# A sixteenth 1 MB buffer for expert weights, in the tiles `ea` and `bg`, loaded in four pieces after the router

## The chip, the cores and the metric

One core of a Trainium2 chip runs the whole program. The metric is device time in microseconds of that core: the median of three runs, beside one more execution that the hardware profiler recorded, on which all rows here are read. The engines are PE (TensorE), DVE (VectorE), ACT (ScalarE), POOL (GpSimd) and SP (SyncE, which in this kernel issues nearly all loads). Each runs its own list of instructions in order, and they meet at semaphores. Sixteen DMA engines move the data.

## The reference

One decoder layer over 536 tokens (512 prompt tokens, 16 meta tokens ahead of them, 8 decode tokens), all in float32: four token mixers, gates and an output projection, and then a mixture of experts. The change touches the last part. Cut to it:

```python
def hier_moe(x, rg_w, rg_b, re_w, re_b, w1, w3, w2):
    pg = jax.nn.softmax((t @ rg_w + rg_b).astype(F32), axis=-1)
    pg_top, g_idx = lax.top_k(pg, 1)
    g_oh = jax.nn.one_hot(g_idx[:, 0], N_GROUPS, dtype=F32)
    le_sel = jnp.einsum('ng,nge->ne', g_oh, le)
    e_val, e_idx = lax.top_k(le_sel, TOP_K_IN)
    wts = jax.nn.softmax(e_val, axis=-1) * pg_top
    ...
    h = jax.nn.silu(jnp.einsum('nd,edf->nef', t, w1)) * jnp.einsum('nd,edf->nef', t, w3)
    h = h * gate[..., None].astype(h.dtype)
    return jnp.einsum('nef,efd->nd', h, w2).reshape(b, l, d)
```

There are 16 experts; w1 and w3 are 1024 x 256 each and w2 is 256 x 1024, so an expert has 3 MB of weights and all have 48 MB. Each of the 520 tokens that have an output goes to two experts.

## The kernel before

The program first projects and mixes, merges the branches, multiplies by the output weights (to 640 us), normalises and routes (to 667 us), and then runs the experts, which is the stage of this change.

**Experts.** They are taken in four quads of four (`QUADS`), a quad in three rounds (`ROUNDS`); a round is one PE tile, in which each expert of the quad has 32 rows of tokens and its own 32 rows of the array. Tokens are gathered by GpSimd from a copy in HBM (`gather`, into `cg`, `sgt`, `dqk`), transposed on PE (`rows_T`, L1198), multiplied by w1 and w3 (`hidden_one`, L1209), passed through silu and product (ACT L1673, DVE L2443), transposed (`hidden_T`, L1261) and multiplied by w2 (`outputs`, L1278, 32 matmuls for each of 3 rounds: 96 for a quad). ACT and DVE copy the result, times its gate, into `cst` (L1683, L2456), and GpSimd adds it to y in HBM, first choices as they come, second choices at the quad's end (L2644).

**Weights.** They are streamed in 48 loads of 1 MB, n = 0 to 47, twelve for a quad: j = n % 12 from 0 to 7 brings w1 and w3, each load for two experts and two of the eight slices of 128 input rows, and j = 8 to 11 brings w2 of one expert. SyncE issues them (`weights`, L505 for a whole MB in one DMA, L508 for the four quarters of a buffer that lies in pieces). With `STREAM` = 15 buffers, load n goes to buffer n % 15. The buffers are no memory of their own: they are tiles of the earlier stages (`kv`, `br`, `sgd` two each, `qb`, `vtok`, `qk` two, `tmp` two, `xn` two, and the fifteenth in four pieces, in `dv`, `vec` and the end of `vtok`), and the first fill has to wait until each tile has been given up. So it is issued in steps: n = 0 to 7 once the merges are done, 8 and 9 after the output product, 14 after two small outputs of the mixers have been stored, 10 and 11 once the first gathers have landed and the transposes out of `tmp` are done, 12 and 13 (in `xn`) once all five blocks of y's residual are stored (`y_out`).

**From n = 15 on** SyncE waits, in order, for the use of load n - 15 (`weights_used`): for the first six of a quad's loads a count that PE gives while it multiplies (`m_use`), for the seventh and eighth the end of the hidden product (`m_h1`), for w2 the end of the outputs (`m_y`). PE's own `weights(n)` waits for the landing (`m_w`).

**Around it.** The five residual blocks are written to y in HBM by SyncE (L521), out of `xn` and of `bg`; the router works in `ea` and `dr` and ends on DVE with the gates of the tiles (`g_w`, L2432), which gives `g_ok`. ACT and GpSimd wait for it too.

Of the kernel before, what the change touches and what calls it, by code (L numbers as in the profile page):

```python
# [14 lines left out]
KT = DM // P  # L15
# [23 lines left out]
RING = 6  # L39
STREAM = 15  # L40
LAST_OUT = [(3, 4), (5, 0), (6, 7)]
# [90 lines left out]
def program(nc, w_in, w_mg, w_dp, w_out, w_13, w_2, x_d, n2_d, xT_d, const_d, vec_d, ret0_d, gla0_d, kc, vc, pt, o):  # L132
    with ExitStack() as ctx:
# [3 lines left out]
        def sem(name):  # L137
            return ctx.enter_context(nc.semaphore(name))
# [15 lines left out]
        bg, cg, dr = sb("bg", 2 * T), sb("cg", 2 * T), sb("dr", 2 * T)  # L154
# [3 lines left out]
        ea = sb("ea", 1024)  # L158
# [124 lines left out]
        slot = [[t[:, g, :] for g in range(4)] for t in slot]  # L283
        slot.append([dv[:, 0:512], dv[:, 512:1024], vec[:, V_WA:V_WA + 512], vtok[:, 2048:2560]])
        xe = [view(t, 0, DM) for t in (cg, sgt, dqk)]
        xeT = [view(ring, DM * i, KT, P) for i in range(2 * ROUNDS)]
# [8 lines left out]
        ld_x, init_ok = [sem(f"ld_xt{i}") for i in range(4)], sem("init_ok")  # L295
# [35 lines left out]
        xs_ok, idx2_ok, oh_ok, oh2_ok, tab_ok, g_ok = [sem(k) for k in ("xs_ok", "idx2_ok", "oh_ok", "oh2_ok", "tab_ok", "g_ok")]  # L331
        m_w = [sem(f"m_w{i}") for i in range(STREAM)]
        m_xe, m_yst = [sem(f"m_xe{i}") for i in range(ROUNDS)], [sem(f"m_yst{i}") for i in range(ROUNDS)]
# [56 lines left out]
        def _(sp):  # L390
# [104 lines left out]
            def weights(n):  # L495
# [6 lines left out]
                w = n % STREAM  # L502
                if w < STREAM - 1:
                    whole = slot_whole[w].rearrange("p (e k) n -> p e k n", e=2) if j < KT else slot_whole[w]
                    sp.dma_start(whole, src).then_inc(m_w[w], 16)  # L505
                else:
                    for g in range(4):
                        sp.dma_start(slot[w][g], src[:, g // 2, g % 2, :] if j < KT else src[:, g, :]).then_inc(m_w[w], 16)  # L508

# [21 lines left out]
            sp.wait_ge(outs, 16 * POOL_OUTS)  # L531
            weights(STREAM - 1)
            for b in range(NB):
# [11 lines left out]
            weights(12)  # L545
            weights(13)
            for n in range(STREAM, 12 * QUADS):
                weights_used(n - STREAM)
                weights(n)
# [17 lines left out]
        def _(pe):  # L567
# [633 lines left out]
            def weights(n):  # L1201
                pe.wait_ge(m_w[n % STREAM], (64 if n % STREAM == STREAM - 1 else 16) * (n // STREAM + 1))
                return slot[n % STREAM]
# [1627 lines left out]
```

## Time and profile before

| | us |
|---|---|
| median of 3 runs | 829.5 |
| lowest, highest | 828.33, 832.01 |
| profiled execution, its own time | 832.47 |
| its span, first to last instruction | 830.7 |
| PE busy in the span | 783.2 (94%) |
| mean granted TensorE clock in the span | 0.969 |

The span is what the rows below are read in: their times count from its start. The rest of the profiled execution's time, 1.8 us, lies around it. A share of busy time says little here: PE is 94% busy over the whole, but what a change to the expert stage is worth is read at that stage's end. In a row of the chain or of a timeline the first number is the start, the second how long it took.

### The profile page before, as it was taken

How to read it: one execution, taken by the hardware profiler on the slowest of the kernel's cores; microseconds unless marked ns; L12 is line 12 of the kernel's file. 1: busy time of each engine (PE TensorE's matmuls, PEld its weight loads, DVE VectorE, ACT ScalarE, POOL GpSimd, SP SyncE). 2: the span in 40 equal slices, each digit the busy share in tenths (PEclk: the TensorE clock that was granted, in tenths of full speed). 3: DMA queues.
4: the chain of work that ended last, by engine and by line, in shares of the span. 5: the costliest groups of instructions: out<-in, count | busy, mean ns of one | idle time of the engine just before them, and what ended most of it. 6: DMA issues, size and time to landing. Idle time of an engine off the chain costs nothing.

```text
span 830.7 us, 14351 instructions
## 1 busy us (share of the span) xinstructions
PE 783.2 (94%) x5282; PEld 560.4 (67%) x5282; DVE 379.7 (46%) x741; ACT 223.7 (27%) x428; POOL 295.4 (36%) x220
## 2 busy tenths in 40 slices
PE   9999999989999999899999999999899799999981
PEld 8887777666667788677777778888688534333320
DVE  4671676767468578444444111635423712022110
ACT  4122424331413634113314224222101512011010
POOL 0000421244663874245435555433240113232313
PEclk9999999999999999899999999999899799999986
DMA  9242632245665542155534553332193779999923
GB/s 368 94 149 87 218 104 78 70 135 159 171 184 171 166 146 64 29 164 165 181 125 135 170 175 129 126 107 81 36 378 133 267 270 408 386 372 386 383 71 48
DMA packets 72154, 147.23 MB, mean 177 GB/s; under 512 B 13207, under 2 KB 47016, under 8 KB 70036
## 3 DMA queue, kind: packets, MB, share of 16 engines
q1 hardware_dynamic: 65716, 135.43, 46.8%
q0 software_dynamic: 5920, 10.82, 5.2%
q8 instruction: 42, 0.69, 0.3%
q14 instruction: 28, 0.23, 0.1%
q10 hardware_dynamic: 448, 0.06, 0.1%
HBM read 137.71 MB, written 18.90 MB: 189 GB/s over the span
## 4 chain that ended last, share of the span: by engine, by line
PE 78%; DVE 9%; SPq 5%; DMA 3%; issue 2%; ACT 2%; POOLq 0%; POOL 0%; ACTq 0%; DVEq 0%
PE ps L875 19%; PE ps L599 13%; PE ps L1209 7%; PE ps L844 6%; PE ps L1117 6%; PE ps L1278 4%; PE ps L614 4%; PE ps L642 3%; DMA br<-in_w 3%; SPq L505 2%; PE ps L899 2%; PE ps L674 2%; PE ps L588 1%; PE ps L1198 1%; PE ps L949 1%
## 5 line engine op out<-in xcount | busy, mean ns | idle before, releaser
L599 PE MATMUL ps<-xn,ring 128*128 128x268 f32 (+1 forms) x576 | 138.4, 395 | 1.0 <-ACT qb L1371 0.9
L599 PEld LDWEIGHTS ps<-xn,ring 128*128 128x128 f32 x576 | 108.2, 192 | 26.1 <-issue 3.4
L2531 POOL TENSOR_TENSOR kv<-kv,sgd 128x1024 f32<-128x1024 f32 (+1 forms) x32 | 81.1, 2548 | 119.7 <-DVE tmp L1820 70.2
L2644 POOL DMA_INDIRECT out_y<-cst,gtab x24 | 37.3, 1555 | 83.5 <-DVE cst L2456 43.2
L1514 ACT ACTIVATE sgt<-sgt,vec 128x260 f32<-128x260 f32 x60 | 30.0, 510 | 134.2 <-DVE sgt L2100 78.0
L844 PE MATMUL ps<-br,ring 128*128 128x260 f32 x256 | 61.7, 389 | 0.8 <-DVE sgt L2104 0.8
L875 PE MATMUL ps<-xn,qb 128*128 128x260 f32 x240 | 59.4, 392 | 0.0
L875 PE MATMUL ps<-xn,ring 128*128 128x260 f32 x240 | 57.9, 384 | 1.0 <-ACT tmp L1371 1.0
L844 PEld LDWEIGHTS ps<-br,ring 128*128 128x128 f32 x256 | 48.3, 192 | 12.1 <-issue 3.7
L875 PEld LDWEIGHTS ps<-xn,qb 128*128 128x128 f32 x240 | 46.5, 194 | 7.5
L875 PEld LDWEIGHTS ps<-xn,ring 128*128 128x128 f32 x240 | 45.1, 190 | 8.3 <-issue 1.4
L1853 DVE TENSOR_REDUCE sgd<-kv 128x32 f32<-128x1024 f32 (+1 forms) x32 | 40.5, 1279 | 9.7 <-POOL kv L2531 9.6
L2091 DVE TENSOR_TENSOR sgt<-ps,sgt 128x260 f32<-128x260 f32 x15 | 6.4, 427 | 71.8 <-PE ps L875 71.8
L2443 DVE TENSOR_TENSOR ring<-ring,ps 128x256 f32<-128x256 f32 x12 | 5.1, 421 | 71.1 <-ACT ring L1673 71.1
L2575 POOL TENSOR_TENSOR qb<-qb,ring 128x512 f32<-128x512 f32 x15 | 19.3, 1286 | 46.4 <-PE ps L875 46.4
L2570 POOL TENSOR_TENSOR qb<-ring 128x512 f32<-128x512 f32 x15 | 20.4, 1360 | 36.8 <-PE ps L875 36.5
L642 PE MATMUL ps<-ring,xn 128*128 128x128 f32 x256 | 31.4, 285 | 0.0
L642 PEld LDWEIGHTS ps<-ring,xn 128*128 128x128 f32 x256 | 30.9, 201 | 0.6 <-ACT tmp L1371 0.3
L2542 POOL TENSOR_TENSOR cst<-sgt,cst 128x520 f32<-128x520 f32 x16 | 20.6, 1289 | 29.7 <-ACTq L1524 29.7
L614 PE MATMUL ps<-kv,ring 128*128 128x268 f32 x128 | 29.9, 394 | 0.0
L1371 ACT ACTIVATE cst<-ps 128x520 f32<-128x520 f32 x32 | 19.3, 603 | 37.7 <-PE ps L844 37.7
L2582 POOL TENSOR_TENSOR qb<-ring,qb 128x512 f32<-128x512 f32 x15 | 19.3, 1287 | 27.8 <-PE ps L875 27.2
(506 smaller groups left out, 1527.4 us busy)
## 6 DMA issues: line engine op xcount, KB each, us to landing
ring<-in_w_mg SPq DMA_DIRECT2D x32, 640.0 KB, 4.7
kv<-in_kc SPq DMA_DIRECT2D x128, 128.0 KB, 2.1
kv<-in_vc SPq DMA_DIRECT2D x128, 128.0 KB, 2.2
ring<-in_w_in SPq DMA_DIRECT2D x24, 512.0 KB, 4.6
kv<-in_w SPq DMA_DIRECT2D x8, 1024.0 KB, 14.9
br<-in_w SPq DMA_DIRECT2D x7, 1024.0 KB, 18.5
sgd<-in_w SPq DMA_DIRECT2D x6, 1024.0 KB, 19.5
qk<-in_w SPq DMA_DIRECT2D x6, 1024.0 KB, 15.5
```

Of the source, the lines that this page charges most:

```text
L599: mm = pe.matmul(ps[:, 2 * (t % 2) + h, 0:hw], wsl(c, k), xnv[:, k, col0 + h * hw:col0 + (h + 1) * hw], start=(k == 0), stop=(k == KT - 1))
L614: mm = pe.matmul(ps[:, EARLY[name] + h, 0:HT], wsl(c, k), xgv[:, k, h * HT:(h + 1) * HT], start=(k == 0), stop=(k == KT - 1))
L642: pe.matmul(ps[:, 2 * (t % 2), b * P:(b + 1) * P], xnv[:, k, b * P:(b + 1) * P], wsl(c, k), start=(k == 0), stop=(k == KT - 1))
L844: mm = pe.matmul(ps[:, bk + h, 0:HN], wsl(CAT[f"G{n}{m}"], KT + k), brv[:, BR[n] + k, h * HN:(h + 1) * HN], start=(k == 0), stop=(k == 1))
L875: mm = pe.matmul(ps[:, bk, 0:HN], w[:, k * P:(k + 1) * P], x, start=(k == 0), stop=(k == 3))
L1117: mm = pe.matmul(ps[:, bk, 0:HN], wk, x, start=(k == 0 and i in (1, 2, 5)), stop=(k == 3), skip_group_check=(i in (6, 7, 4, 3)))
L1209: mm = pe.matmul(ps[rows, i % ROUNDS, :], xeT[i % (2 * ROUNDS)][:, k, rows], slot[(i // ROUNDS * 12 + k - k % 2 + g // 2) % STREAM][2 * (g ...
L1278: mm = pe.matmul(ps[rows, LAST_OUT[r][n] if last else 6 + n, :], hT[r][:, f, rows], w[g][2 * f + n], start=(f == 0), stop=(f == 1), tile_p ...
L1514: act.activation(g, g, ACT.Sigmoid, bias=vv(V_BM + 8 * "ABCD".index(n) + m + i)).then_inc(g_a, 1)
L1853: dve.tensor_reduce(row, kb.rearrange("p s (m d) -> p s m d", d=32), X, ALU.add).then_inc(k_used, 1)
L2531: pool.tensor_tensor(kb, kb, qbc[:, b:b + 1, :].to_broadcast([P, HALF // 2 + (half and u), 256]), ALU.mult)\
L2644: pool.indirect_dma_start(out=o["y"], out_offset=on_rows(to), in_=rows.rearrange("p a n -> p (a n)"), in_offset=None, bounds_check=N - 1, ...
```

## The change

`STREAM` becomes 16, and the number of whole buffers gets a name of its own, `WHOLE` = 14. The fifteenth buffer (index 14) stays as it is, and a sixteenth (index 15) is added, in four pieces of 256 KB: both halves of `ea`, where the decays of mixer D's gates and later the router's numbers were, and the first 1024 columns of `bg`, B's gate and later the fifth residual block. Load n = 15 is now part of the first fill. It is issued after n = 12 and 13, behind the wait for `y_out`, and behind one new wait of SyncE, for `g_ok`. From n = 16 on SyncE waits for the use of n - 16. The landing of the new buffer is counted on an old semaphore, `ld_x[0]`, which stands at 16 since the first load of the input, so PE's wait adds that base.

```diff
--- before.py
+++ after.py
@@ -37,7 +37,7 @@
 RB = N // NB
 WCH = 1280
 RING = 6
-STREAM = 15
+WHOLE, STREAM = 14, 16
 LAST_OUT = [(3, 4), (5, 0), (6, 7)]
 OUT_ORDER = [1, 5, 6, 2, 7, 3, 4]
 OUT_BANKS = [(6, 7, 3), (0, 1, 2)]
@@ -282,6 +282,7 @@
         slot_whole = slot
         slot = [[t[:, g, :] for g in range(4)] for t in slot]
         slot.append([dv[:, 0:512], dv[:, 512:1024], vec[:, V_WA:V_WA + 512], vtok[:, 2048:2560]])
+        slot.append([ea[:, 0:512], ea[:, 512:1024], bg[:, 0:512], bg[:, 512:1024]])
         xe = [view(t, 0, DM) for t in (cg, sgt, dqk)]
         xeT = [view(ring, DM * i, KT, P) for i in range(2 * ROUNDS)]
         si = [view(ring, 6 * DM + 256 * i, 256) for i in range(ROUNDS)]
@@ -329,7 +330,7 @@
         rw_ok, lg_t, lg_a, lg_d = sem("rw_ok"), sem("lg_t"), sem("lg_a"), sem("lg_d")
         r1, r2, sel_ok, idx_ok = sem("r1"), sem("r2"), sem("sel_ok"), sem("idx_ok")
         xs_ok, idx2_ok, oh_ok, oh2_ok, tab_ok, g_ok = [sem(k) for k in ("xs_ok", "idx2_ok", "oh_ok", "oh2_ok", "tab_ok", "g_ok")]
-        m_w = [sem(f"m_w{i}") for i in range(STREAM)]
+        m_w = [(sem(f"m_w{i}"), 0) for i in range(STREAM - 1)] + [(ld_x[0], 16)]
         m_xe, m_yst = [sem(f"m_xe{i}") for i in range(ROUNDS)], [sem(f"m_yst{i}") for i in range(ROUNDS)]
         m_t, m_ta, m_td, m_h1, m_si, m_h = [sem(f"m_{k}") for k in ("t", "ta", "td", "h1", "si", "h")]
         m_ht, m_htev, m_y, m_ya, m_yd, m_use = [sem(f"m_{k}") for k in ("ht", "htev", "y", "ya", "yd", "use")]
@@ -500,12 +501,12 @@
                 else:
                     src = w_2[4 * q + j - KT, :, :, :].rearrange("p f (h n) -> p (f h) n", h=2)
                 w = n % STREAM
-                if w < STREAM - 1:
+                if w < WHOLE:
                     whole = slot_whole[w].rearrange("p (e k) n -> p e k n", e=2) if j < KT else slot_whole[w]
-                    sp.dma_start(whole, src).then_inc(m_w[w], 16)
+                    sp.dma_start(whole, src).then_inc(m_w[w][0], 16)
                 else:
                     for g in range(4):
-                        sp.dma_start(slot[w][g], src[:, g // 2, g % 2, :] if j < KT else src[:, g, :]).then_inc(m_w[w], 16)
+                        sp.dma_start(slot[w][g], src[:, g // 2, g % 2, :] if j < KT else src[:, g, :]).then_inc(m_w[w][0], 16)
 
             def weights_used(n):
                 q, j = n // 12, n % 12
@@ -529,7 +530,7 @@
             weights(8)
             weights(9)
             sp.wait_ge(outs, 16 * POOL_OUTS)
-            weights(STREAM - 1)
+            weights(WHOLE)
             for b in range(NB):
                 sp.wait_ge(tt_a, b + 1)
                 sp.dma_start(scr_x[b * RB:(b + 1) * RB, :], tk[b]).then_inc(xs_ok, 16)
@@ -544,6 +545,8 @@
             sp.wait_ge(y_out, 16 * NB)
             weights(12)
             weights(13)
+            sp.wait_ge(g_ok, 1)
+            weights(STREAM - 1)
             for n in range(STREAM, 12 * QUADS):
                 weights_used(n - STREAM)
                 weights(n)
@@ -1199,7 +1202,8 @@
                 mm.then_inc(m_t, 1)
 
             def weights(n):
-                pe.wait_ge(m_w[n % STREAM], (64 if n % STREAM == STREAM - 1 else 16) * (n // STREAM + 1))
+                s, base = m_w[n % STREAM]
+                pe.wait_ge(s, base + (16 if n % STREAM < WHOLE else 64) * (n // STREAM + 1))
                 return slot[n % STREAM]
 
             def hidden_one(i, k):
```

On SyncE, from the loads behind `y_out` to those of quad 2. Names are destination tiles; `xn` is n = 12 and 13. Before:

```order
L505 DMA xn<-in_w 128x2x1024 [waits y_out]
L505 DMA xn<-in_w 128x2x1024
L505 DMA kv<-in_w 128x2x1024 [waits m_use] x2
L505 DMA br<-in_w 128x2x1024 [waits m_use] x2
L505 DMA sgd<-in_w 128x2x1024 [waits m_use]
L505 DMA sgd<-in_w 128x2048 [waits m_use]
L505 DMA qb<-in_w 128x2048 [waits m_h1]
L505 DMA vtok<-in_w 128x2048 [waits m_h1]
L505 DMA qk<-in_w 128x2048 [waits m_y]
L505 DMA qk<-in_w 128x2x1024 [waits m_y]
```

After, from the same place on:

```order
L506 DMA xn<-in_w 128x2x1024 [waits y_out]
L506 DMA xn<-in_w 128x2x1024
L509 DMA ea<-in_w 128x512 [waits g_ok]
L509 DMA ea<-in_w 128x512
L509 DMA bg<-in_w 128x512 x2
L506 DMA kv<-in_w 128x2x1024 [waits m_use] x2
L506 DMA br<-in_w 128x2x1024 [waits m_use] x2
L506 DMA sgd<-in_w 128x2048 [waits m_use] x2
L506 DMA qb<-in_w 128x2048 [waits m_h1]
L506 DMA vtok<-in_w 128x2048 [waits m_h1]
L506 DMA qk<-in_w 128x2x1024 [waits m_y] x2
```

The four pieces of n = 15 (`ea`, `bg`) stand between `xn` and `kv`, `kv` now takes n = 16 and 17, and the first load that waits for a quad's outputs (`m_y`) is n = 24, the first of `qk`, where it was n = 23, the same buffer.

At the end of SyncE's loads, the last rows (n = 44 to 47 among them). Before:

```order
L505 DMA xn<-in_w 128x2x1024 [waits m_use] x2
L508 DMA dv<-in_w 128x512 [waits m_use]
L508 DMA dv<-in_w 128x512
L508 DMA vec<-in_w 128x512
L508 DMA vtok<-in_w 128x512
L505 DMA kv<-in_w 128x2048 [waits m_h1] x2
L505 DMA br<-in_w 128x2048 [waits m_y]
```

After:

```order
L506 DMA xn<-in_w 128x2048 [waits m_use] x2
L509 DMA dv<-in_w 128x512 [waits m_h1]
L509 DMA dv<-in_w 128x512
L509 DMA vec<-in_w 128x512
L509 DMA vtok<-in_w 128x512
L509 DMA ea<-in_w 128x512 [waits m_h1]
L509 DMA ea<-in_w 128x512
L509 DMA bg<-in_w 128x512 x2
```

Before (the first row there is n = 42 and 43), n = 44 went in pieces, n = 45 and 46 to `kv` and n = 47 to `br`, the last behind the outputs of quad 2. After, n = 44 and 45 are whole, in `xn` (the first row), and n = 46 and 47 are eight pieces behind the end of quad 2's hidden product. In all six loads go in pieces (n = 14, 15, 30, 31, 46, 47), where three did (14, 29, 44): 12 DMAs more. On PE only the tiles that the matmuls read change, not their order or number.

## Rows read from the trace of the kernel before

**Rows 1.** Chain that ended last: start us, us, what; times merged.

```profile
733.68 7.00 PE ps L1278 x64
...
779.06 20.82 DMA br<-in_w
...
800.23 13.43 PE ps L1278 x96
```

**Rows 2.** PE's timeline at the last outputs, then its waits from 668 us on.

```profile
796.99 0.44 PE L1261 MATMUL ps<-cst,ring 128*128 128x128 f32 x2 [0.37 <-DVE ring L2443]
800.23 1.03 PE L1278 MATMUL ps<-dv,cx 128*32 128x512 f32 x1 [2.80 <-DMA br<-in_w]
...
PE ps L1278 <- DMA br<-in_w: 2.8, 1, 2.8
```

**Rows 3.** Stretches: busy us (x instructions) by engine, PEclk, DMA share, GB/s.

```profile
792.00:796.00 4.00, 4.00 (x41) 1.07 (x33) 0.76 (x2) 0.77 (x2) 0.00 (x0) 1.00 0.49 124
796.00:800.00 4.00, 1.06 (x10) 0.58 (x6) 1.50 (x5) 0.38 (x1) 0.00 (x0) 0.91 0.10 29
800.00:804.00 4.00, 3.77 (x20) 1.12 (x24) 0.00 (x0) 0.07 (x1) 0.00 (x0) 0.50 0.02 4
```

**Rows 4.** DMA, 682 to 783 us: busy tenths in 40 slices; an issue group.

```profile
DMA  6999999999999999999999999999999999999999
...
vtok<-in_w SPq DMA_DIRECT2D x2, 256.0 KB, 16.5
```

**Rows 5.** SyncE's waits, 668 to 706 us: us in total, times, longest.

```profile
SPq L505 <- PE ps L1278: 12.6, 1, 12.6
SPq L505 <- DMA out_y<-bg: 11.0, 1, 11.0
```

**Rows 6.** SyncE's timeline: start us, us, line, op, tiles, count.

```profile
681.98 0.92 SPq L505 DMA_DIRECT2D xn<-in_w  x2
682.95 1.48 SPq L505 DMA_DIRECT2D kv<-in_w  x2
...
692.32 1.06 SPq L505 DMA_DIRECT2D vtok<-in_w  x1
...
716.29 5.12 SPq L508 DMA_DIRECT2D dv<-in_w  x2
...
725.06 4.29 SPq L505 DMA_DIRECT2D kv<-in_w  x2
...
768.02 4.17 SPq L508 DMA_DIRECT2D dv<-in_w  x2
...
774.47 1.07 SPq L508 DMA_DIRECT2D vtok<-in_w  x1
775.58 3.43 SPq L505 DMA_DIRECT2D kv<-in_w  x2
779.06 3.44 SPq L505 DMA_DIRECT2D br<-in_w  x1
```

**Rows 7.** VectorE's timeline at the instruction that signals `g_ok`.

```profile
666.95 0.18 DVE L2432 TENSOR_TENSOR dr<-dr 128x22 f32<-128x22 f32 x1
```

**Rows 8.** Landings of the loads issued at 692.32, 765.66, 774.47, 775.58.

```profile
DMA to landing us min/median/max: 25.8/25.8/25.8
...
L505 SPq DMA_DIRECT2D xn<-in_w x1: 2310/2310/2310, 765.7 to 765.7; - x1
...
DMA to landing us min/median/max: 21.6/21.6/21.6
...
DMA to landing us min/median/max: 15.5/15.5/15.5
...
DMA to landing us min/median/max: 17.1/17.1/17.1
```

**Rows 9.** Landing of GpSimd's addition (L2644) of 720.09, ScalarE's next write.

```profile
DMA to landing us min/median/max: 9.1/9.1/9.1
...
731.00 0.69 ACT L1683 ACTIVATE cst<-ps,dr 128x512 f32<-128x512 f32 x1 [1.72 <-PE ps L1278]
```

## Prediction

> **What bounds the kernel now.** I read the views backwards from the end. The chain that ended last [rows 1] says what the last stretch hangs on: the load of w_2 into `br`, issued at 779.06 us, lands 20.82 us later, at 799.88, and only then do the 96 matmuls of the last outputs (L1278) run, until 813.66. PE's timeline and waits [rows 2] give the size of that wait. The last transposes of the hidden rows end at 796.99 + 0.44 = 797.43 us, and the engine then stood 2.80 us, until 800.23. The wait costs a second time. The granted clock is 0.91 in 796 to 800 and 0.50 in 800 to 804 [rows 3], which is the 1.2 GHz level after a stretch in which PE was busy for 1.06 of 4 us; so the 96 matmuls took 13.43 us, where 64 of them took 7.00 at the full level [rows 1], which makes 10.5 for 96. That is 2.93 us. Everything that can be had at the end is 2.80 + 2.93 = 5.7 us, and nothing else in the expert stage waits for a weight: in PE's waits from 668 us on this is the only one on a load from the weights [rows 2].
>
> So the time is set by when the 48th MB lands, and the question is what sets that. The DMA view of 682 to 783 us [rows 4] answers it: in 40 slices of 2.5 us the engines are busy 6 tenths in the first and 9 tenths or more in the 39 others. The queue drains without a pause from about 684.5 to about 792 us. In the last 8 us the mean share of the 16 engines is 0.49 and then 0.10 [rows 3]: most of them have ended, and a few are still bringing their share of the last MBs. The last landing is therefore the time at which the fullest engine has moved all that it was given, and it was never without work since 684.5.
>
> **The change part by part.**
>
> *The first load of the new buffer.* n = 15 goes to the sixteenth buffer, where it waited for `kv` to be used. But both versions issue it behind the same wait, for all five stores of y. SyncE stood 11.0 us on the last of them, `out_y<-bg` [rows 5], until 681.98. Then come n = 12 and 13, and n = 15 went out at 682.95, with no wait worth a row before it [rows 6]: `kv` was already free. The new wait on `g_ok` costs nothing: the VectorE instruction that gives it (L2432) starts at 666.95 and takes 0.18 us [rows 7], 15 us before SyncE comes to it. After the change n = 15 goes out at about 682.95 again, in four pieces, into a queue that has 2 MB in front of it. Gain: 0. The hole in the DMA engines' work lies before 681.98, and the new load stands behind it as all others do. The most that more loads at this place can fill is the rest of that first slice, 0.4 x 2.5 = 1.0 us. I take 0, because two loads are in front either way and the slice is the start of the first one (nothing can land before 688.6).
>
> *The waits that become shorter.* From n = 16 on each load waits for the use of n - 16 instead of n - 15. The large ones are at the borders of a quad. Before, n = 23 waited for the end of the outputs of quad 0, 12.6 us [rows 5], from 692.32 + 1.06 = 693.4 [rows 6] to 706.0; now it waits for h1 like its neighbour n = 22, goes out at about 694, and the 12.6 us wait falls on n = 24. What does it bring? The `vtok` load of 692.32 landed 25.8 us later, at 718.1 [rows 8], so when SyncE woke at 706.0 the queue had 12 us of work left. A load that is issued 12 us earlier into a queue that is 25 us deep lands at the same time: the order of the bytes is the same, and so is the engines' rate. Gain: 0. The same holds at the next border (n = 35) and at the last one, where n = 47 waited for the outputs of quad 2 and now waits for h1. Before, the two `kv` issues ahead of it ended at 775.58 + 3.43 = 779.01 and it followed at 779.06 [rows 6]: it did not wait for the outputs, it stood behind the slow issues of a full queue. Gain: 0.
>
> *The pieces.* Three buffers' worth went in pieces (n = 14, 29, 44), now six (14, 15, 30, 31, 46, 47): 12 DMA issues more on SyncE, which does nothing else there. What a MB in pieces costs the DMA engines can be read at n = 43 to 45. The last whole load of `xn` (issued 765.66) landed after 21.6 us, at 787.3; the last piece of n = 44 (`vtok`, 774.47) after 15.5, at 790.0; the whole n = 45 (`kv`, 775.58) after 17.1, at 792.7 [rows 6, 8]. That is 2.7 us for the MB in pieces and 2.7 for the whole one behind it: cost 0 for each. On SyncE a MB in pieces took 725.06 - 716.29 = 8.8 us [rows 6], and 7.6 from 768.02 to 775.58, against some 2.2 for a whole one, all of it with a full queue. I read this as the queue pushing back, since the DMA share does not fall in those slices. If it were the pieces' own price, it would be the upper bound below.
>
> The Trainium skill speaks against the pieces ("DMA: Bandwidth & Descriptors", sections "Anatomy of one DMA" and "Bandwidth"): it gives each transfer a fixed cost of about 2.0 us and advises 1 MiB or more for each. By that fit, an estimate for transfers made one after the other, four pieces would cost 3 x 2.0 = 6.0 us more than a whole, and three such MBs 18 us. The spacing of the landings above, 2.7 against 2.7, says that in a backlogged queue nothing of it is paid.
>
> *Those who share the engines.* A deeper queue could hold up GpSimd's gathers and its additions to y. The tightest place is the second addition of quad 0, which starts at 720.09 and landed after 9.1 us, at 729.2; ScalarE overwrites its source at 731.00 [rows 9]: 1.8 us of slack. While SyncE's loads needed 14 to 26 us, the addition needed 9.1, so it does not stand behind them, and one MB more there does not move it. If it did, by the 2.7 us of a MB, the stall would be 0.9 us, once in a quad, and beside PE's work. Taken: 0.
>
> *The sum.* 0 (first load) + 0 (waits) + 0 (pieces) + 0 (sharing) = no change. The unknown ends are -1.0 (first slice) and +0.9. The profiled execution took 832.47 us with a span of 830.7, which is 3.0 above the median of 829.5; I apply the sum to the median: **829.5 us**.
>
> **The rivals.**
>
> *The last load comes in time (faster).* If the deeper run-ahead, or another spread over the engines, lets the last MB land before 797.43 instead of 799.88, 2.5 us earlier, PE loses both the wait and the low clock: 829.5 - 5.7 = 823.8. For it: only a few engines were busy after 792, so a small shift in the distribution would do, and the last two loads change from whole ones to pieces. Against it: no byte is issued into an idle engine that wasn't before, except for the 1.0 us of the first slice, and 2.5 are needed. A partial one (1 us earlier, clock still lost) lies within 0.5%. Chance 0.13.
>
> *The pieces' issue sets the end (slower).* n = 46 and 47 are now eight issues at the very end. If 2.2 us each (8.8 / 4) is their own price and not the queue's, then with n = 44 and 45 whole at 768.0 and 770.2 the pieces start at 772.4, the last goes out at 772.4 + 7 x 2.2 = 787.8, and with the 16.5 us that a `vtok` piece took from issue to landing [rows 4] it lands at 804.3, 4.4 later than before: 829.5 + 4.4 = 833.9, and more if the clock stays low longer. It decides from the point at which the last piece goes out after 799.9 - 16.5 = 783.4. For it: the pace in rows 6, and the skill's rule. Against it: at the loads of n = 29 and 44 the engines stayed full during those slow issues. Chance 0.11.
>
> *The buffer never fills anything* is not a rival but my forecast: the change does what it says, SyncE runs a MB further ahead, and the engines that move the bytes are no faster. Chance 0.76.
>
> **How the numbers follow.** About 0.5%, 4.1 us, is what a measurement of this kernel can tell from no change; the three runs shown differ by 3.7. Forecast 0.76 within it; faster 0.13 and slower 0.11 are the two rivals. The forecast's own range is 829.5 - 1.0 and + 0.9, widened by the runs' own spread of 1.2 below and 2.5 above the median: 827.3 to 832.9. To hold 8 in 10 it has to reach some way toward both rivals: **825.0 to 834.0**.
>
> **What would show it right or wrong.** In the changed kernel's profile: SyncE's wait of about 11 us for `out_y<-bg` and the first `xn` load at about 682 again; `ea` and `bg` pieces right behind, from about 682.9; a wait of about 12 us before n = 24 instead of n = 23; all slices of the DMA view from 684.5 to 790 at 9; the last load landing at 799 to 801 us; a PE wait of 2 to 4 us before the last L1278 and the clock at 0.50 behind it. It is wrong if the last landing moves by more than 2 us either way, if the DMA share between 700 and 790 falls under 0.95, or if PE waits for a weight anywhere else.

## The result and the profile after

The changed kernel takes **831.7 us** (median of 14 runs, 826.5 to 836.9), the kernel before 828.2 us in 14 runs beside it (825.0 to 832.0). The ratio is **1.0042, with a 95% interval of 1.0024 to 1.0061**: 3.5 us slower. That is inside the half per cent that the forecast called no change and inside its range of 825 to 834, but the interval leaves 1 out, so a small loss has to be explained where the forecast had exactly nothing. The kernel before is a little faster than the three runs shown at first (829.5), and the execution whose profile stands ahead of the prediction (832.5 us) turns out to be longer than its usual one. That matters below.

The profiled execution of the changed kernel took 830.4 us, with a span of 828.7. SyncE's waits from 668 to 707 us come first (us in total, times, longest); they answer to [rows 5].

```profile
SPq L506 <- PE ps L1282: 11.6, 1, 11.6
SPq L506 <- DMA out_y<-bg: 11.4, 1, 11.4
```

SyncE's timeline (start us, us, line, operation, tiles, count), to be read against [rows 6]:

```profile
682.25 0.93 SPq L506 DMA_DIRECT2D xn<-in_w  x2
683.22 1.24 SPq L509 DMA_DIRECT2D ea<-in_w  x2
684.51 1.17 SPq L509 DMA_DIRECT2D bg<-in_w  x2
685.72 0.99 SPq L506 DMA_DIRECT2D kv<-in_w  x2
...
692.59 1.60 SPq L506 DMA_DIRECT2D vtok<-in_w  x1
705.84 0.90 SPq L506 DMA_DIRECT2D qk<-in_w  x2
...
772.71 2.68 SPq L509 DMA_DIRECT2D dv<-in_w  x2
775.42 2.35 SPq L509 DMA_DIRECT2D vec<-in_w  x1
777.82 1.20 SPq L509 DMA_DIRECT2D vtok<-in_w  x1
779.06 3.16 SPq L509 DMA_DIRECT2D ea<-in_w  x2
782.26 4.92 SPq L509 DMA_DIRECT2D bg<-in_w  x2
```

The change does what it says. The wait for the last store of y is as long as before (11.4 us), the new buffer's four pieces follow right behind n = 12 and 13, and the wait for quad 0's outputs (11.6 us, until 705.8) has moved from n = 23 to n = 24. The DMA engines of 682 to 783 us, as in [rows 4]:

```profile
DMA  5999999999999999999999999999999999999999
```

No gap anywhere, again. The end: the chain of waits (start us, us, what), PE's timeline, PE's waits from 668 us on, and the stretches (busy us by engine, PEclk, DMA share, GB/s), which answer to [rows 1 to 3].

```profile
785.07 14.47 DMA bg<-in_w
...
799.89 12.24 PE ps L1282 x96
```

```profile
796.84 0.44 PE L1265 MATMUL ps<-cst,ring 128*128 128x128 f32 x2 [0.37 <-DVE ring L2447]
799.89 0.62 PE L1282 MATMUL ps<-xn,cx 128*32 128x512 f32 x2 [2.61 <-DMA bg<-in_w]
...
PE ps L1282 <- DMA bg<-in_w: 2.6, 1, 2.6
```

```profile
792.00:796.00 4.00, 4.00 (x41) 1.10 (x31) 0.84 (x2) 0.82 (x3) 0.00 (x0) 1.00 0.65 155
796.00:800.00 4.00, 1.02 (x10) 0.57 (x13) 1.42 (x4) 0.33 (x1) 0.00 (x0) 1.00 0.14 54
800.00:804.00 4.00, 4.00 (x28) 1.35 (x29) 0.00 (x0) 0.69 (x1) 0.00 (x0) 0.64 0.01 4
```

PE still waits for one weight only, the last, now 2.61 us. These two profiles alone would say that nothing happened: the last load is at 799.5 after and 799.9 before. So the loss is not in this pair of traces, and has to be found with more executions of both kernels.

### The profile page after: what moved, and what is told of

Read it like the earlier page. It is cut to its first block, busy times and chain, and to the rows that moved or that the text cites. A ratio compares the mean times of both kernels' runs of the same rounds, so it can differ in the third digit from the quotient of the medians.

```text
span 828.7 us, 14360 instructions
## 1 busy us (share of the span) xinstructions
PE 779.8 (94%) x5282; PEld 558.2 (67%) x5282; DVE 379.9 (46%) x741; ACT 223.7 (27%) x428; POOL 294.9 (36%) x220
## 4 chain that ended last, share of the span: by engine, by line
PE 78%; DVE 9%; DMA 4%; SPq 4%; issue 2%; ACT 2%; POOLq 0%; POOL 0%; ACTq 0%; DVEq 0%
PE ps L878 20%; PE ps L602 13%; PE ps L1213 7%; PE ps L847 7%; PE ps L1120 6%; PE ps L1282 4%; PE ps L645 3%; PE ps L617 3%; PE ps L902 2%; SPq L506 2%; PE ps L677 2%; DMA bg<-in_w 2%; PE ps L591 1%; SPq L509 1%; PE ps L1201 1%
## 5 line engine op out<-in xcount | busy, mean ns | idle before, releaser
L602 PE MATMUL ps<-xn,ring 128*128 128x268 f32 (+1 forms) x576 | 136.7, 392 | 1.0 <-ACT qb L1375 0.9
```

The source lines that it names most:

```text
L602: mm = pe.matmul(ps[:, 2 * (t % 2) + h, 0:hw], wsl(c, k), xnv[:, k, col0 + h * hw:col0 + (h + 1) * hw], start=(k == 0), stop=(k == KT - 1))
```

## A yardstick

Two things vary from execution to execution whatever the kernel. The first is when the expert stage's stream starts behind its hole, which is the first issue of `xn` (681.98 before, 682.25 after); over the runs below it lies anywhere from 678.8 to 685.4 us, because of the work ahead of it. The second is whether PE's last wait costs the granted clock. So I read each trace from the first issue of `xn` to the landing of the last load, and apart from it PE's last wait and the time of the 96 matmuls behind it.

| kernel, execution | first `xn` | last landing, after `xn` | PE's last wait | the 96 matmuls |
|---|---|---|---|---|
| before, shown ahead of the prediction | 681.98 | 117.9 | 2.80 | 13.43 |
| before, e5 | 684.78 | 115.8 | 1.50 | 12.24 |
| before with 12 met waits, e6 | 678.84 | 115.7 | none | 10.54 |
| before, e15 | 680.46 | 115.7 | 0.90 | 10.54 |
| changed, shown above | 682.25 | 117.3 | 2.61 | 12.24 |
| changed, e7 | 681.54 | 117.7 | 2.94 | 12.24 |
| changed, e13 | 683.67 | 117.4 | 2.50 | 13.50 |

The landing is taken as the start of the first of the 96 matmuls less the 0.35 us that the chain puts between the two (in e6, where PE waited for VectorE instead, from the load's own record, 794.49). Of the kernel before, three of four executions have the last load 115.7 to 115.8 us behind the first `xn`; the one on which the prediction rests has 117.9. The changed kernel has 117.3 to 117.7 in all three. The likely reading is that **the last load lands some 1.6 us later after the change than it usually did before**. It rests on seven executions and on calling the 117.9 unusual; with it in the mean the difference is 1.2 us. The wait is 2.7 us on the mean of three, against 1.3 of four, and the 96 matmuls take 12.7 against 11.7. Together that is 2.4 us. The three timings of the changed kernel (1.0042, and 1.0004 and 1.0052 below) have a mean of 1.0033, or 2.7 us. The size fits; how much of it repeats is the first thing to test, and then which part of the change it comes from.

The usual end of the kernel before, in e15 (SyncE's timeline, then the chain):

```profile
680.46 1.05 SPq L505 DMA_DIRECT2D xn<-in_w  x2
...
775.68 20.50 DMA br<-in_w
...
796.53 10.54 PE ps L1278 x96
```

## The experiments

Ratios are to the kernel before, timed on the same chip in the same batch, with 95% intervals. Four chips were used, called A to D here; that turned out to matter. My theory at the start: the pieces at the end land the last weight later. Its rivals: the changed waits of SyncE, the issues' own price on SyncE at the end, and no effect at all.

### The depth of the run-ahead

`e1_wait15` is the changed kernel with the old depth: each load waits for the use of n - 15, as before, and the sixteenth buffer stays.

```diff
             for n in range(STREAM, 12 * QUADS):
-                weights_used(n - STREAM)
+                weights_used(n - STREAM + 1)
                 weights(n)
```

> The changed kernel, but from n = 16 on SyncE waits for the use of load n - 15, as before the change, so that it runs no further ahead than before; buffers and pieces are those of the changed kernel. If the pieces cost the 3.5 us (theory P), they are all here: 1.003 to 1.006 of the kernel before. If running a MB further ahead costs them (theory D: a deeper queue holds up others), nothing is left: 0.998 to 1.002.

Measured on chip A: 1.0045 [1.0026, 1.0064], the changed kernel's own ratio. Its chain:

```profile
785.36 14.46 DMA bg<-in_w
...
800.18 11.87 PE ps L1282 x95
```

The last load lands 117.3 us behind the first `xn` (682.56). So running one load further ahead is not what costs the 3.5 us. By itself it neither helps nor costs anything that this timing can tell, as the prediction had it.

`e4_fourteen` goes the other way: fourteen whole buffers, no pieces at all.

```diff
-STREAM = 15
+STREAM = 14
...
-        slot.append([dv[:, 0:512], dv[:, 512:1024], vec[:, V_WA:V_WA + 512], vtok[:, 2048:2560]])
...
-            weights(STREAM - 1)
```

> The kernel before without its fifteenth buffer: 14 whole buffers, no load in pieces, SyncE a MB less far ahead. If the engines' backlog hides depth (my prediction) and pieces cost (P-all): three MBs in pieces fewer, 0.994 to 0.998, unless the hole before 682 us grows by the MB that is no longer loaded at 640 us; that MB (2.6 us of the engines' time) moves behind the hole, which by itself makes 1.003. Together about 1.000. D: 0.996 to 0.999 with the same 1.003 against it.

Measured on chip A: 1.0050 [1.0028, 1.0073]. Chain and PE's timeline:

```profile
776.89 25.66 DMA sgd<-in_w
...
802.91 12.24 PE ps L1276 x96
```

```profile
802.91 1.01 PE L1276 MATMUL ps<-br,cx 128*32 128x512 f32 x2 [4.45 <-DMA sgd<-in_w]
```

The last landing is 119.3 us behind the first `xn` (683.30), although nothing is in pieces. The fifteenth buffer is first filled *ahead* of the hole (behind the wait for `outs`); without it one more MB has to come behind the hole, and a MB costs 2.7 us there. That is most of the 3.5 us by which this landing is later than the usual 115.8; three MBs in pieces fewer should have made it less, and this rest is open. So a buffer is worth its first fill, if that falls before the hole. The sixteenth's first fill falls behind it.

### The pieces

`e3_tail_pieces` makes the other half of the change alone: the kernel before, fifteen buffers, with n = 46 and 47 in four DMAs each.

```diff
                 w = n % STREAM
-                if w < STREAM - 1:
+                if w < STREAM - 1 and n < 46:
...
-                pe.wait_ge(m_w[n % STREAM], (64 if n % STREAM == STREAM - 1 else 16) * (n // STREAM + 1))
+                pe.wait_ge(m_w[n % STREAM], (64 if n % STREAM == STREAM - 1 else 16) * (n // STREAM + 1) + (48 if n >= 46 else 0))
```

> The kernel before (15 buffers), but n = 46 and 47 are loaded by four DMAs of 256 KB each into their whole buffers: six DMAs more, all at the end. P-end: 1.003 to 1.006, like the changed kernel. P-all: two of the three added MBs in pieces, so 1.002 to 1.004. D: 0.998 to 1.002.

Measured on chip A: 1.0046 [1.0025, 1.0067], the whole loss of the change. It was run a second time:

> The kernel before with n = 46 and 47 in four pieces each, again, beside the changed kernel. If pieces at the end are what counts, it equals the changed kernel; if all three added MBs count alike, it has two thirds of its cost: 1.001 to 1.002.

Again on chip A: 1.0035 [1.0016, 1.0053]. The last landings are 117.1 us behind the first `xn` in both, 1.4 more than the usual 115.7.

`e2_swap_end` asks whether it is their place at the very end: the changed kernel with the buffers of the last four loads exchanged, so that n = 44 and 45 go in pieces and n = 46 and 47 whole to `xn`.

```diff
+        def buf(n):
+            return {44: 14, 45: 15, 46: 12, 47: 13}.get(n, n % STREAM)
...
-                weights_used(n - STREAM)
+                weights_used({44: 30, 45: 31, 46: 28, 47: 29}.get(n, n - STREAM))
```

> The changed kernel with the last four loads in another order of buffers: n = 44 and 45 go in pieces (dv/vec/vtok and ea/bg), n = 46 and 47 whole into xn. Pieces as many as in the changed kernel, but none at the very end. If pieces at the end set the last landing (theory P-end), the time returns to that of before, 0.998 to 1.002. If every MB in pieces costs the same wherever it stands (P-all) or if depth costs (D), it stays at 1.003 to 1.006.

Measured on chip A: 1.0040 [1.0015, 1.0066], last landing at 116.9. Here the last issue is a whole load, and the loss stays, so it isn't that the pieces are the very last. By itself this does not clear SyncE: the eight pieces still stand ahead of the last issue, which goes out 101.4 us behind the first `xn` (786.40 - 685.03), where `e15` has 95.2. `e10` below settles it.

`e17_mid_pieces` puts eight pieces in the middle (n = 24 and 25) of the kernel before, with the same kind of edit as `e3`.

> The kernel before with the loads n = 24 and 25 in four pieces each, in the middle of the stream, where the run with pieces at the end had n = 46 and 47. If pieces cost by their number alone, it equals that run: 1.003 to 1.005. If their place at the end is what costs, 1.000 to 1.002.

Measured on chip D: 1.0002 [0.9977, 1.0027], last landing at 116.4. By itself this reads as "pieces in the middle cost nothing". But its last landing is 0.7 us behind the usual, half of what `e3` shows, and it ran on another chip than `e3`, and the chips differ by as much (below). The loads differ too: n = 24 and 25 bring w1 and w3, whose whole loads have rows of 4 KB (128x2x1024), n = 46 and 47 bring w2 with rows of 8 KB (128x2048), and in pieces both have 2 KB (128x512). Whether the place counts is not settled.

`e9_all_pieces` multiplies the suspect: in the kernel before every load from n = 15 on goes in four pieces, 31 MBs more than before and 93 more DMAs.

```diff
-                if w < STREAM - 1:
+                if w < STREAM - 1 and n < STREAM:
...
-                pe.wait_ge(m_w[n % STREAM], (64 if n % STREAM == STREAM - 1 else 16) * (n // STREAM + 1))
+                pe.wait_ge(m_w[n % STREAM], (64 if n % STREAM == STREAM - 1 else 16) + 64 * (n // STREAM))
```

> The kernel before (15 buffers, same waits), but every load from n = 15 on goes as four DMAs of 256 KB with 2 KB rows: 31 MBs more in pieces than before, where the change has 3 more. If a MB in pieces costs the DMA engines something (theory P), this multiplies it by ten: at 0.3 us for each, 9 us, 1.008 to 1.015; at 1.2 us for each, which the 3.5 us of the first timing would mean, 36 us, 1.03 and more. If it costs nothing, 0.998 to 1.002.

Measured on chip C: 1.0097 [1.0068, 1.0125]. DMA engines of 682 to 783 us, chain, and PE's waits from 668 us on:

```profile
DMA  4999999999999999999999999999999999999999
```

```profile
794.50 9.40 DMA br<-in_w
...
804.26 12.88 PE ps L1278 x96
```

```profile
PE ps L1278 <- DMA br<-in_w: 4.9, 1, 4.9
PE ps L1278 <- DMA sgd<-in_w: 2.0, 1, 2.0
```

This is the clearest result of all. Pieces have a price in a full queue: 8.1 us for 31 MBs by the timing, 0.26 us each. By the trace the last landing comes 121.6 us behind the first `xn` (682.30), 5.9 more than usual, or 0.19 us each. The 0.26 has the end's costs in it: the 96 matmuls take 12.88 us here, 1.2 more than the mean of 11.7 above. (The wait of 2.0 for `sgd` falls at the outputs of the third quad, about 768 us, not at the end.) And the engines are shown busy all the time: the price is paid *inside* the busy tenths, as a lower rate, and can't be seen in that view. (The few MBs in the list that were in pieces before, n = 29 and 44, are not counted.)

The queue's own line does show it. SyncE's queue from 682 to 783 us (packets, MB, the time that its packets took as a share of 16 engines), first before, then in `e9`:

```profile
q1 hardware_dynamic: 8074, 33.31, 81.9%
```

```profile
q1 hardware_dynamic: 16635, 31.41, 83.7%
```

That is 0.819 x 101 / 33.31 = 2.48 us of the mean engine for a MB before and 2.69 in `e9`, 0.21 more. There are also twice as many packets, because every split of these runs shortens the rows as well, to 2 KB. The trace's packets bear on which of the two counts: from 684 to 780 us in `e15` a packet of 8 KB takes 312 ns on the mean, one of 4 KB 162 and one of 2 KB 85. From these, an estimate: a MB in rows of 2 KB takes 512 x 85 / 16 = 2.72 us of the mean engine, against 2.59 in rows of 4 KB and 2.50 in rows of 8 KB, so 0.13 and 0.22 more. The three further DMAs of a split MB add 48 packets of 4 bytes at 10 ns, 0.03 us. So by this estimate the shorter rows are the larger part of the price and the number of DMAs the smaller. No run splits a load without shortening its rows.

`e10_halves` reduces it: the changed kernel with the two halves of `dv`, of `ea` and of `bg` loaded by one DMA each, so that the six MBs take 15 DMAs instead of 24.

```diff
+PARTS = [[(0, 2), (2, 1), (3, 1)], [(0, 2), (2, 2)]]
...
-                    for g in range(4):
-                        sp.dma_start(slot[w][g], src[:, g // 2, g % 2, :] if j < KT else src[:, g, :]).then_inc(m_w[w][0], 16)
+                    for g, k in PARTS[w - WHOLE]:
...
+                        sp.dma_start(to, of).then_inc(m_w[w][0], 16)
```

> The changed kernel, but the pieces that lie side by side are loaded by one DMA with 4 KB rows: ea and bg as two halves, dv as one. 15 DMAs instead of 24 for the six MBs. Theory P: between before and after, 1.000 to 1.002. Theory that the first fill behind the wait for y gives nothing and all else is free: 0.998 to 1.002.

Measured on chip C: 1.0031 [1.0012, 1.0050], last landing at 116.9. Between the change and nothing, but the intervals overlap with the change's; it doesn't decide what the pieces cost. It does decide about SyncE. Its last issue goes out 95.7 us behind the first `xn` (777.04 - 681.31), as early as in the kernel before (95.2 in `e15`, 95.9 in `e5`), and the last landing is late all the same. So the pace at which SyncE issues the pieces, the slower rival of the prediction, doesn't set the end.

### The same kernels again, and on other chips

`e5_null` and `e15_null_again` are the kernel before against itself, on chips B and A; `e7_after_again` and `e13_after_third` the changed kernel.

> The kernel before, unchanged, timed against itself. It gives the size of a difference that means nothing, and a second profiled execution of the kernel before: 0.998 to 1.002. If it comes out at 1.003 or more, the differences of all variants so far are no property of their edits.

Chip B: 0.9996 [0.9976, 1.0016].

> The kernel before against itself again: 0.999 to 1.001, and a third profiled execution of it.

Chip A: 0.9995 [0.9977, 1.0013]. So the comparison of two equal kernels gives 1, within 0.2%.

> The changed kernel again, for a second profiled execution and on the same chip as the controls: 1.003 to 1.006.

Chip B: **1.0004 [0.9982, 1.0026]**, no loss at all.

> The changed kernel a third time. If its cost is that of three more MBs in pieces (0.8 us by the run with all in pieces) and what the low clock adds to it: 1.001 to 1.003. If the first timing's 0.42% is a property of the change: 1.004. If it is nothing: 0.999 to 1.001.

Chip A: **1.0052 [1.0028, 1.0077]**. The same kernel loses on one chip and not on the other, by one timing on B, whose interval just reaches that of the first timing (1.0024). Its last landing and PE's wait are no better on B (117.7 and 2.94) than on A (117.4 and 2.50). Both kernels differ in the median: the one before takes 829.95 us in 35 runs on chip B and 828.2 to 828.7 on A, and the changed one 830.1 on B and 833.8 on A. (The record names no chip for the first timing, 1.0042, in which it took 831.7.) Each run also gives the mean granted clock over its span:

| | chip A, before | chip A, changed | chip B, before | chip B, changed |
|---|---|---|---|---|
| median, us | 828.7 | 833.8 | 830.0 | 830.1 |
| runs | 35 | 12 | 35 | 12 |
| mean of the granted clock | 0.9740 | 0.9702 | 0.9729 | 0.9736 |
| runs with less than 0.973 | 11 | 9 | 20 | 4 |

On chip A the changed kernel has the low clock in three of four runs and the one before in one of three; on B the one before has it in more than half. Over the 35 runs on each chip the time of the kernel before and this clock have a correlation of -0.81 and -0.83. A longer wait lowers the mean and a lower clock lengthens the run, so the number doesn't say which comes first. It doesn't say either where the clock is lost. `e8` below has 0.970 in its profiled execution, and its last 96 matmuls take 10.5 us, at 2.4 GHz; `e7` has 0.975, and they take 12.24. In the clock records of the twenty traces the low clock takes away 10 to 19 us of full clock ahead of the first `xn` and 6 to 11 behind it, so most of this number is made ahead of the stage that the change touches. The table shows that time and clock go together; it can't explain by the last wait why chip B shows no loss, and that stays open.

`e6_waits` adds twelve waits that are already met (`y_out`, from n = 36 on) to SyncE in the kernel before, as a control for instructions on SyncE at the end.

```diff
             for n in range(STREAM, 12 * QUADS):
+                if n >= 36:
+                    sp.wait_ge(y_out, 16 * NB)
                 weights_used(n - STREAM)
```

> The kernel before with twelve more waits on SyncE, ahead of the loads n = 36 to 47, for a condition that has long been met. No load, byte or buffer differs. Theory P (the pieces cost) and D: 0.998 to 1.002. If any edit of SyncE's list shifts the time (theory A: where the instructions lie, or how SyncE's list is fetched), 1.003 to 1.005.

Chip B: 1.0005 [0.9985, 1.0026]. SyncE's instructions cost nothing, as the prediction had it.

### What the last load is worth, and what moves it forward

`e8_no_last` leaves the 48th load out, so that PE can't wait for it; the matmuls of that expert read what lies in its buffer.

```diff
-            for n in range(STREAM, 12 * QUADS):
+            for n in range(STREAM, 12 * QUADS - 1):
...
+                if n < 12 * QUADS - 1:
```

> The kernel before without the 48th load: n = 47 is not loaded and PE does not wait for it; the matmuls of that expert's w2 read what lies in its buffer, so one expert's outputs are wrong in this run. If the engines' total work sets the end, the last landing comes 2.5 us earlier, at the time when PE is ready, so PE's wait shrinks to 0 to 1 us: 2.5 us from the wait and up to 2.9 us from the clock, 0.993 to 0.997. If the end is set by something else, 0.998 to 1.002.

Chip B: 0.9980 [0.9961, 0.9998], 1.7 us. PE's waits from 668 us on hold no load of weights any more, and the 96 matmuls take 10.5 us. The prediction had 5.7 us for "everything that can be had at the end", from its one execution; by this timing it is less than a third of that (0.2 to 3.2 us by the interval).

`e11_early_kv` makes use of it: the kernel before, with n = 15 and 16 (to `kv`, which is free early) issued *before* SyncE's wait for the five stores of y and before n = 12 and 13, so that the hole ends earlier.

```diff
                 residual(b)
+            weights_used(0)
+            weights(STREAM)
+            weights_used(1)
+            weights(STREAM + 1)
             sp.wait_ge(y_out, 16 * NB)
             weights(12)
             weights(13)
-            for n in range(STREAM, 12 * QUADS):
+            for n in range(STREAM + 2, 12 * QUADS):
```

> The kernel before (15 buffers), but the loads n = 15 and 16 (into kv, free at 679.7 us in the trace of before) are issued ahead of the wait for y and of n = 12 and 13, whose buffers that wait is for. It moves the end of the hole in the engines' work from 682.0 to 679.7. If the end is set by when the engines' unbroken work begins, the last landing comes 2.3 us earlier, and PE loses 2.3 us of wait and up to 2.9 us of low clock: 0.994 to 0.997. If not: 0.999 to 1.001.

Chip C: **0.9970 [0.9948, 0.9991]**, 827.0 us. SyncE's and PE's timelines:

```profile
683.33 0.92 SPq L505 DMA_DIRECT2D kv<-in_w  x2
684.36 1.23 SPq L505 DMA_DIRECT2D xn<-in_w  x2
```

```profile
799.47 0.59 PE L1282 MATMUL ps<-dv,cx 128*32 128x512 f32 x1 [0.24 <-DVE cx L2452]
```

The stream starts only 1.0 us ahead of `xn`, since `kv` itself waits for its use as n = 0 and 1, and that is enough: PE's last wait is on VectorE and the 96 matmuls take 10.54 us. Once more, on chip D:

> The kernel before with n = 15 and 16 ahead of the wait for y, a second time, on another chip or day: 0.995 to 0.999, as the first time. If that was chance: 0.999 to 1.001.

0.9984 [0.9951, 1.0018], 826.6 us against 829.4, with the same end (PE waits 0.29 us, 10.54 for the 96). Twice in the same direction, once with 1 outside the interval: a version that beats the kernel before by 0.2 to 0.3%, and so probably the changed one too; they were not timed against each other, nor was this one on a chip on which the change was timed.

`e12_sixteen_early` joins everything that looked good: sixteen buffers, the larger DMAs of `e10`, `kv` early, and one half of the sixteenth buffer (`ea`) already behind the router.

```diff
                 residual(b)
+            sp.wait_ge(g_ok, 1)
+            weights(STREAM - 1, PARTS[1][:1])
+            weights_used(0)
+            weights(STREAM)
+            weights_used(1)
+            weights(STREAM + 1)
             sp.wait_ge(y_out, 16 * NB)
...
-            sp.wait_ge(g_ok, 1)
-            weights(STREAM - 1)
+            weights(STREAM - 1, PARTS[1][1:])
```

> Sixteen buffers, halves as in the run before last, n = 16 and 17 (kv) ahead of the wait for y, and the first half of n = 15 (ea) right after the router, at about 670 us, where the engines were busy for half of the time; its second half (bg) after the wait. Against the 15 buffers with early kv it brings half a MB, 1.3 us, into the hole: 0.992 to 0.997. If PE's own work then sets the end, no more than 0.993.

Chip C: 0.9986 [0.9963, 1.0008], no better than `e11`. Its stretches (as above), then PE's timeline:

```profile
668.00:682.00 14.00, 14.00 (x129) 5.36 (x125) 1.80 (x3) 2.86 (x4) 1.99 (x2) 1.00 0.94 347
...
792.00:796.00 4.00, 2.76 (x25) 0.88 (x14) 2.26 (x6) 1.15 (x3) 0.00 (x0) 1.00 0.12 31
796.00:800.00 4.00, 1.59 (x8) 0.45 (x12) 0.00 (x0) 0.00 (x0) 0.00 (x0) 0.57 0.03 10
```

```profile
798.41 1.07 PE L1293 MATMUL ps<-xn,cx 128*32 128x512 f32 x2 [3.28 <-DMA bg<-in_w]
```

The hole is nearly filled (share 0.94 from 668 to 682 us; 0.85 in e15). Most engines are done soon after 792, and yet PE waits 3.28 us, until 798.4. At a mean share of 0.12 and 0.03, two engines' worth and then half an engine's, what is waited for is one or two engines of the sixteen.

The same can be read in the changed kernel's issues (tiles, count, size, median us from issue to landing) from 760 to 790 us:

```profile
ea<-in_w SPq DMA_DIRECT2D x2, 256.0 KB, 10.5
bg<-in_w SPq DMA_DIRECT2D x2, 256.0 KB, 13.9
```

The four pieces of n = 47 count on one semaphore, 16 each, so "the first piece's landing" is the time when 16 of 64 engine shares are in, whichever pieces they belong to. In the changed kernel that is at 789.85, half of them at 791.17, three quarters at 795.62 and all at 799.54. The last of n = 46 comes only at 797.02, 7 us after 16 shares of n = 47 are in, so some engines are well into the next load while another still works on the one before. The landings of `e14` show the same four steps (789.7, 790.9, 795.4, 799.3). A whole load shows the engines one by one, as I read the 16 steps in which its semaphore counts: n = 47 in the trace of the kernel before has its first step at 787.69, the eighth at 791.08, the fifteenth at 797.00 and the last at 799.88, 12 us from first to last (in `e15` 784.86, 789.77, 795.47 and 796.18). It also shows what was unusual in that execution: its last engine came 2.9 us behind the fifteenth, in `e5`, `e6` and `e15` 0.5 to 1.4.

`e16_fetches` tried one idea of why some engines lag: that they also fetch the instructions of the compute engines. It adds 256 semaphore increments to each of ScalarE's quads 1 to 3 in the kernel before.

```diff
                 i, more = ROUNDS * q, q < QUADS - 1
+                if q:
+                    for _ in range(256):
+                        act.sem_inc(lam_e, 1)
```

> The kernel before with 256 semaphore increments on ScalarE ahead of its silus in each of the quads 1 to 3, where it waits 20 us for PE anyway. No load differs; the program is 768 instructions longer, so that more of it has to be fetched by DMA in the expert stage. If the DMA engine that fetches instructions is the slowest one that sets the last landing, and three fetches more cost it 1 us each: the last landing is 2 to 4 us later, 1.004 to 1.008. If the fetches go to engines with time left: 0.999 to 1.002, or a little more if ScalarE comes late.

Chip A: 1.0029 [1.0006, 1.0052], last landing at 116.8. Something of it may reach the end, but the increments also delay ScalarE, so it proves little. Why some DMA engines lag stays open.

## Why the prediction was right and wrong

**What bounds the kernel: right for the changed kernel.** The last weight's landing does set the end in all three executions of it that were profiled, and in three of the four of the kernel before (in `e6` PE doesn't wait for it), and the start of that stream goes far to set the landing. Moving the start by 1 us (`e11`) is worth more than a sixteenth buffer.

**First load and waits, 0: right.** SyncE's rows are where they were foretold (682.25, pieces from 683.22, 11.4 and 11.6 us of waits), and `e1` shows nothing gained or lost by the depth itself, in a queue that is never empty. `e4` shows under which condition a buffer would be worth something.

**Sharing, 0: nothing seen against it.** PE has no wait for anything but the last load (its second is 0.8 us), and this was not tested by itself.

**The pieces, 0: the step that failed, as a mis-sized term.** The text read 2.7 us for the MB in pieces and 2.7 for the whole one behind it, and concluded "cost 0 for each". `e9` gives 0.26 us for each MB by the timing and 0.19 by the trace. One spacing can't show that: whole MBs near the end land 2.5 to 4.4 us apart in these traces, and each landing is that of the slowest engine alone (in n = 45 it came 2.8 us behind the fifteenth). Three more MBs in pieces should cost 0.6 to 0.8 us at the last landing; 1.4 was seen where only two more went in pieces at the end (`e3`, `e14`), and some 1.6 for the change. So the pieces alone bring the loss on chip A (`e3`, `e14`), but only half of its size follows from the price for each MB; whether the other half belongs to the pieces' place near the end, to the longer rows that w2 loses, or to the scatter of single executions is not shown. The Trainium skill's fixed cost ("DMA: Bandwidth & Descriptors", section "Anatomy of one DMA"), which the prediction set aside, has the right sign. By the fit given there, which is for DMAs that GpSimd issues, an estimate for `e9`'s 93 further DMAs made one after another is 186 us, where the runs show 8.1; the measurement decides.

**One execution was taken for the usual one: the second part of the miss.** The prediction saw a kernel that already waits 2.80 us and has already lost the clock, so that a small shift of the landing seemed to cost only itself, and a gain seemed worth 5.7 us. In two of the three other executions PE waits 0.9 us or not at all for that load, and the 96 matmuls take 10.54 us, the time at 2.4 GHz. There a landing that comes 1.6 us later costs the wait and, in some executions, 1.3 to 3 us of clock on top (11.8 to 13.5 against 10.54). This is how 1.6 us at the landing can become 2.4 at the end of the profiled executions and 2.7 on the mean of three timings; it is read from three executions against four. It doesn't explain chip B, where the changed kernel's profile (`e7`) has the same late landing (117.7), wait (2.94) and loss of clock (12.24), and its timing shows no loss.

**The rivals.** "The last load comes in time" didn't happen; it needed bytes issued into an idle engine, and `e11` and `e18` show the form in which it does. "The pieces' issue sets the end" has the direction and nearly the size (833.9 forecast, 831.7 measured), but not the mechanism: the last piece went out at 785.07, where 787.8 was forecast, and in `e10`, where the last issue goes out as early as before the change, the last landing is late all the same. The price lies with the DMA engines, not on SyncE. The pace of [rows 6] was the queue pushing back: `dv`'s pieces took 2.68 us for two in a full queue, and `ea`'s 1.24 in an empty one.

**The chances.** "Within 0.5%" is what happened, by 0.1%. But costs that were all put at exactly 0, with bounds of -1.0 and +0.9, left the pieces no price at all beyond the slower rival, where `e9` shows one; the slower side should have held more than 0.11.

## What to carry to other kernels

A further buffer of prefetch is worth what its *first* fill moves into time in which the DMA engines would idle, and nothing if the queue is already full behind it; look for what starts the stream earlier instead. Splitting transfers isn't free in a backlogged queue, even when every slice of the view shows the engines busy: count about a quarter of a microsecond per MB in four pieces, and keep the rows long: here they went from 4 or 8 KB to 2 KB with the split, and the estimate from the packets' times puts most of the price there. When a stage ends in a wait of 1 to 3 us that sometimes costs the clock, profile several executions before pricing anything there, measure from the start of the stream and not in absolute time, and repeat a result of 0.4% on a second chip.

## What was not expected of the hardware

- A MB in four DMAs of 256 KB instead of one costs 0.19 to 0.26 us in a full queue (`e9`), with the DMA engines' share at 9 tenths or more either way. Packets of 8, 4 and 2 KB take 312, 162 and 85 ns (`e15`), so the same MB takes the engines longer in shorter rows.
- The 16 DMA engines don't end together: the 16 steps of one whole MB (n = 47, before) come from 787.69 to 799.88 us, and the last load is waited for at a mean share of 0.03 to 0.14.
- The same 96 matmuls took 10.54 us after waits of 0 to 1.94 us, and 11.8 to 13.5 after waits of 1.5 to 4.9 us; in the stretch behind the wait the granted clock is 0.64 in the changed kernel. Between 1.5 and 1.94 us of wait both outcomes occur (`e5` and `e17` against `e3` and `e10`).
- The same pair of kernels gives 1.0042 and 1.0052 in two timings and 1.0004 on another chip, while a kernel against itself gives 0.9996 and 0.9995.
